# A two-layer transformer kernel: order of the wide weight products, sorted gate and up slots, S5 outputs a slot later, one mask product, and attention's sums by high and low parts

## The reference, cut to what matters

```python
def swiglu(x, w_gate, w_up, w_down):
    return (jax.nn.silu(x @ w_gate) * (x @ w_up)) @ w_down
...
# stick_breaking_attention, 8 heads of 128
z = jnp.einsum('bthd,bshd->bhts', qf[:, q0:kend], kf[:, :kend])
causal = s_idx < t_idx
log_beta = jax.nn.log_sigmoid(z)
log_one_minus = jnp.where(causal, log_beta - z, 0.0)
rest = lax.cumsum(log_one_minus, axis=3, reverse=True) - log_one_minus
w = jnp.where(causal, jnp.exp(log_beta + rest), 0.0)
outs.append(jnp.einsum('bhts,bshd->bthd', w, vf[:, :kend]))
...
# s5_mixer
_, hstate = lax.associative_scan(combine, (a, bu), axis=1)
y = (jnp.einsum('gpn,blgn->blgp', c_re, hstate.real) - jnp.einsum('gpn,blgn->blgp', c_im, hstate.imag) + d_skip * uf)
y = jax.nn.gelu(y.reshape(bsz, L, S5_WIDTH))
y = y * jax.nn.sigmoid(y @ w_glu + b_glu)
```

## Time and profile before

| | |
|---|---|
| median of 3 runs | 1508.41 us (1508.37 to 1508.93) |
| the profiled execution: its time | 1510.64 us |
| its span, first to last instruction | 1508.8 us |
| TensorE matmul busy, share of the span | 1499.7 us, 99% |
| TensorE weight load | 1388.6 us, 92% |
| VectorE (DVE) | 1182.3 us, 78% |
| ScalarE (ACT) | 792.6 us, 53% |
| HBM read | 258.61 MB, 172 GB/s over the span |

### The profile page before, as it was taken

The page is one execution under the profiler, slowest core; times in us unless marked ns, Lnnn a source line. Parts: engine busy times, 40 slices in busy tenths (PEclk is TensorE's granted clock), DMA queues, the critical chain, the costliest instruction groups (busy, mean ns, idle before and its releaser), DMA issues.

```text
span 1508.8 us, 25562 instructions
## 1 busy us (share of the span) xinstructions
PE 1499.7 (99%) x10908; PEld 1388.6 (92%) x10908; DVE 1182.3 (78%) x1560; ACT 792.6 (53%) x1003; POOL 39.4 (3%) x41
## 2 busy tenths in 40 slices
PE   8999999999999999999999999999999999999999
PEld 7888899999988888888889999999999999999989
DVE  7987776797888865988758688889998899766744
ACT  6444455565544443544445556455545745775654
POOL 0000001210000000000001020000000000000000
PEclk9999999999999999999999999999999999999999
DMA  7555545434555545555554444465554453325531
GB/s 283 196 196 195 175 167 184 153 140 150 186 185 187 190 173 200 191 180 185 191 191 149 174 151 157 143 227 194 197 194 172 164 193 131 125 106 189 182 126 56
DMA packets 38976, 261.30 MB, mean 173 GB/s; under 512 B 4688, under 2 KB 5584, under 8 KB 9168
## 3 DMA queue, kind: packets, MB, share of 16 engines
q1 hardware_dynamic: 38000, 258.62, 47.8%
q10 hardware_dynamic: 864, 1.05, 0.2%
HBM read 258.61 MB, written 1.05 MB: 172 GB/s over the span
## 4 chain that ended last, share of the span: by engine, by line
PE 94%; DVE 4%; ACT 1%; DMA 0%; issue 0%; ACTq 0%
PE ps L264 22%; PE ps L211 14%; PE ps L213 14%; PE ps L212 14%; PE ps L266 11%; PE ps L725 8%; PE ps L727 4%; DVE w_low L201 2%; PE ps L1448 1%; DMA w_raw<-in_weights 0%; PE ps L1439 0%; PE ps L1421 0%; ACT w_high L194 0%; DVE scratch L2119 0%; PE ps L1463 0%; PE ps L2264 0%
## 5 line engine op out<-in xcount | busy, mean ns | idle before, releaser
L194 ACT ACTIVATE w_high<-w_raw 128x2048 fp32r<-128x2048 f32 (+2 forms) x244 | 459.8, 1886 | 423.2 <-PE ps L266 188.1
L201 DVE TENSOR_TENSOR w_low<-w_raw,w_high 128x2048 fp32r<-128x2048 f32 (+2 forms) x244 | 552.8, 2267 | 127.3 <-ACT w_high L194 125.3
L264 PE MATMUL ps<-x,w_high 128*128 128x512 f32 x1408 | 498.4, 399 | 2.5 <-DVE w_low L878 2.5
L266 PE MATMUL ps<-x,w_low 128*128 128x256 f32 x1408 | 394.8, 280 | 0.0
L264 PEld LDWEIGHTS ps<-x,w_high 128*128 128x128 f32 x1408 | 265.2, 188 | 67.2 <-DVE x L817 2.8
L266 PEld LDWEIGHTS ps<-x,w_low 128*128 128x128 f32 x1408 | 266.3, 189 | 0.1
L211 PE MATMUL ps<-x,w_high 128*128 128x256 f32 x904 | 261.0, 289 | 0.2 <-DVE x L302 0.2
L213 PE MATMUL ps<-x,w_low 128*128 128x256 f32 x904 | 255.7, 283 | 0.0
L212 PE MATMUL ps<-x,w_high 128*128 128x256 f32 x904 | 255.6, 283 | 0.0
L725 PE MATMUL ps<-ffn_hid,w_high 128*128 128x512 f32 x528 | 183.2, 390 | 0.0
L211 PEld LDWEIGHTS ps<-x,w_high 128*128 128x128 f32 x904 | 173.1, 192 | 5.1 <-issue 3.9
(11 more groups left out here) (456 smaller groups left out, 2359.4 us busy)
## 6 DMA issues: line engine op xcount, KB each, us to landing
w_raw<-in_weights SPq DMA_DIRECT2D x231, 1024.0 KB, 4.8
w_raw<-in_weights SPq DMA_DIRECT2D x10, 768.0 KB, 4.2
w_raw<-in_weights SPq DMA_DIRECT2D x5, 512.0 KB, 3.8
even_second_vectors<-in_second SPq DMA_DIRECT2D x1, 1836.0 KB, 7.2
resid<-in_x SPq DMA_DIRECT2D x3, 256.0 KB, 6.5
w_raw<-in_weights ACTq DMA_DIRECT2D x3, 256.0 KB, 8.0
out<-resid SPq DMA_DIRECT2D x3, 256.0 KB, 2.4
table<-in_table SPq DMA_DIRECT2D x1, 737.0 KB, 8.3
```

Source lines behind the costliest of these rows:

```text
L194: act.activation(self.wh[:, j, 0:SIZES[n]], self.raw[:, j, 0:SIZES[n]], ACT.Copy).then_inc(self.hi_made, 1)
L201: dve.tensor_tensor(self.wl[:, j, 0:SIZES[n]], self.raw[:, j, 0:SIZES[n]], self.wh[:, j, 0:SIZES[n]].bitcast(F32), ALU.subtract).then_inc( ...
L264: pe.matmul(c.bank(bank + i).rearrange("p (a t) -> p a t", a=2), wh[:, k, f], c.x[:, :, k, :], start=(k == 0), stop=False, skip_group_chec ...
L266: mm = pe.matmul(c.bank(bank + i, SEQ), wl[:, k, f], c.xh[:, k, :], start=False, stop=(k == DT - 1), skip_group_check=True)
```

## The change

1. `wide`: a slot without a norm, from the third slot on, first runs its 16 matmuls of `w_high` (512 columns) and then its 16 of `w_low` (256 columns). It waits for `hi_made` before the first half and for `lo_made` before the second; `midway` is run between the halves.
2. `A_Y`: the first two S5 outputs move one slot back, from behind slots 6 and 8 to behind 7 and 9.
3. `scores`: the two mask products of 128 columns a head become one of 256.
4. `suffixes`: DVE's `lost` now also makes a high and a low part of the lost part (two more instructions, the first behind a wait for the previous pair's sums); the constant matrices are copied once into fp32r (`tri`, `minus`, two more DVE instructions). A head's sums are six fp32r matmuls in place of three float32 ones (six in the profile).
5. `suffixes(p)` moves from behind slot 15 + p into the middle of slot 16 + p, behind `spread`; ACT does `logs` before `weights`.
6. The low part uses the room of `yl`, so `gelu_low` waits for the last pair's sums, and it stands behind `after(n)` and `attention_low` in DVE's iteration 18.

```diff
--- before.py
+++ after.py
@@ -245,7 +245,23 @@
 def wide(c, pe, bank, n, norm=None, midway=None):
 
 
     wh, wl = c.weights_at(n, DT, FC)
+    if n > 1 and not norm:
+        pe.wait_ge(c.hi_made, c.made(n))
+        for k in range(DT):
+            for i in range(2):
+                pe.matmul(c.bank(bank + i).rearrange("p (a t) -> p a t", a=2), wh[:, k, i * P:(i + 1) * P], c.x[:, :, k, :],
+                          start=(k == 0), stop=False, skip_group_check=True)
+        pe.wait_ge(c.lo_made, c.made(n))
+        for k in range(DT):
+            if midway and k == 0:
+                midway()
+            for i in range(2):
+                mm = pe.matmul(c.bank(bank + i, SEQ), wl[:, k, i * P:(i + 1) * P], c.xh[:, k, :], start=False,
+                               stop=(k == DT - 1), skip_group_check=True)
+        return mm
     if n > 1:
         pe.wait_ge(c.lo_made, c.made(n))
     for k in range(DT):
@@ -1716,7 +1732,7 @@
 A_ATT, A_SUFFIX, A_PV = 14, 15, 17
 A_S5 = (2, 3, 5, 6, 8, 9, 11, 12)
 A_IN = {2: (0, 2), 5: (2, 2), 8: (4, 1), 9: (5, 1), 11: (6, 1), 12: (7, 1)}
-A_Y = (6, 8, 11, 14)
+A_Y = (7, 9, 11, 14)
 QK_SLOTS, PAIRS = 8, SB_HEADS // 2
 
 EVEN_UNITS = ([(n, 0, "dve") for n in range(A_V)] + [(n, 0, "act") for n in range(A_V, A_GLU)]
@@ -1753,6 +1769,7 @@
         self.decay, self.turn, self.gain = sb("decay", [P, S5_TILES]), sb("turn", [P, S5_TILES]), sb("gain", [P, DT])
         self.qg, self.half_bg = sb("q_gain", [P, 1]), sb("half_b_glu", [P, UT])
         self.ident, self.mask = sb("ident", [P, P], F32R), sb("mask", [P, 2, P], F32R)
+        self.tri, self.minus = sb("tri", [P, P], F32R), sb("minus", [P, P], F32R)
         self.ss = sb("q_sums", [P, 2, 4])
         self.mix, self.first = sb("both_means", [P, SEQ]), sb("first_rstd", [P, SEQ])
         self.cos = sb("cos", [P, S5_TILES, HALF])
@@ -1773,6 +1790,7 @@
         logs = (self.rot[:, 0:6 * P], self.b[:, :, :, :].rearrange("p a c n -> p (a c n)")[:, 0:6 * P])
         self.logs = [t.rearrange("p (h t) -> p h t", h=2) for t in logs]
         self.w = [self.cos[:, 6 * i:6 * i + 6, :].rearrange("p a t -> p (a t)").rearrange("p (h t) -> p h t", h=2) for i in range(2)]
+        self.lost = [t.rearrange("p a t -> p (a t)")[:, 0:6 * P].rearrange("p (h t) -> p h t", h=2) for t in (self.obh, self.yl)]
         self.gate = self.rot[:, :].rearrange("p (a t) -> p a t", a=UT)
         self.vec_in, self.gain_made, self.sq_made, self.sum_made, self.mix_made, self.rooted, self.first_made, self.h_made = (
             c.sem(f"even_{n}") for n in ("vec_in", "gain_made", "sq", "sum", "mix_made", "first_root", "first", "resid_normed"))
@@ -1824,6 +1842,8 @@
             dve.tensor_scalar(e.qg[:, :], E[:, E_QG:E_QG + 1], SB_SCALE, None, ALU.mult)
             dve.tensor_scalar(e.half_bg[:, :], E[:, E_BG:E_BG + UT], 0.5, None, ALU.mult)
             dve.tensor_scalar(e.ident[:, :], c.tab[:, T_IDENT:T_IDENT + P], 1.0, None, ALU.mult)
+            dve.tensor_scalar(e.tri[:, :], c.tab[:, T_TRI:T_TRI + P], 1.0, None, ALU.mult)
+            dve.tensor_scalar(e.minus[:, :], c.ones[:, 4, :], 1.0, None, ALU.mult)
             dve.tensor_scalar(e.mask[:, :, :], c.tab[:, T_STRICT:T_STRICT + P].unsqueeze(1).to_broadcast([P, 2, P]), 1.0, -NEG,
                               ALU.subtract, ALU.mult)
             dve.tensor_tensor(e.gain[:, :], c.vec[:, V_N1:V_N1 + DT], E[:, E_NORM:E_NORM + DT], ALU.mult).then_inc(e.gain_made, 1)
@@ -2046,10 +2066,10 @@
                 value(n)
             if 0 <= n - A_ATT < PAIRS:
                 act.preload_act_table_set("natural_log_exp_and_others")
+            if 0 <= n - A_ATT < PAIRS:
+                logs(n - A_ATT)
             if 0 <= n - A_SUFFIX < PAIRS:
                 weights(n - A_SUFFIX)
-            if 0 <= n - A_ATT < PAIRS:
-                logs(n - A_ATT)
             if n == A_GLU - 2:
                 gelu()
             if 0 < n < A_GLU - 1:
@@ -2132,10 +2152,13 @@
         def lost(p):
 
 
-            l = e.logs[p % 2]
+            l, (high, low) = e.logs[p % 2], e.lost
             dve.wait_ge(self.logged, p + 1)
-            dve.scalar_tensor_tensor(out=l, in0=self.score_banks(p), scalar=0.0, in1=l, op0=ALU.max,
-                                     op1=ALU.add).then_inc(self.lost_made, 1)
+            ln(dve.scalar_tensor_tensor(out=l, in0=self.score_banks(p), scalar=0.0, in1=l, op0=ALU.max, op1=ALU.add))
+            if p:
+                dve.wait_ge(self.suffix_made, p)
+            ln(dve.tensor_scalar(high, l, 1.0, None, ALU.mult))
+            dve.tensor_tensor(low, l, high.bitcast(F32), ALU.subtract).then_inc(self.lost_made, 1)
 
         def gated(p):
             h = slice(2 * p, 2 * p + 2)
@@ -2162,6 +2185,7 @@
 
         def gelu_low():
             dve.wait_ge(self.y_high, 1)
+            dve.wait_ge(self.suffix_made, PAIRS)
             dve.tensor_tensor(e.yl[:, :, :], e.u[:, :, :], e.yh[:, :, :].bitcast(F32), ALU.subtract).then_inc(self.y_low, 1)
             dve.wait_ge(self.y_low, 1)
             ln(dve.scalar_tensor_tensor(out=e.u[:, :, :], in0=e.u[:, :, :], scalar=0.5, in1=e.zb, op0=ALU.mult, op1=ALU.mult))
@@ -2185,14 +2209,14 @@
                 gated(n - A_PV)
             if 0 <= n - A_ATT < PAIRS:
                 lost(n - A_ATT)
-            if n == A_GLU - 2:
-                gelu_low()
             if n:
                 after(n)
             if n in A_S5 and n != A_Q:
                 scan(A_S5.index(n))
             if n >= A_PV:
                 attention_low(n - A_PV)
+            if n == A_GLU - 2:
+                gelu_low()
             if n == A_V - 1:
                 self.norm.first(dve)
             if n in (A_V, A_V + 1):
@@ -2295,20 +2319,29 @@
                 h, z = 2 * p + i, self.score_banks(p)[:, i, :]
                 pe.matmul(z[:, 0:SEQ], e.k[:, h, 0:P], e.q[:, h, :], start=True, stop=False, skip_group_check=True)
                 pe.matmul(z[:, SEQ:3 * P], e.k[:, h, P:SEQ], e.q[:, h, P:SEQ], start=False, stop=False, skip_group_check=True)
-                for a in range(2):
-                    mm = pe.matmul(z[:, 2 * a * P:(2 * a + 1) * P], e.ident[:, :], e.mask[:, a, :], start=False, stop=False,
-                                   skip_group_check=True)
+                mm = pe.matmul(z.rearrange("p (a t) -> p a t", a=3)[:, 0:3:2, :], e.ident[:, :], e.mask[:, :, :], start=False,
+                               stop=False, skip_group_check=True)
             mm.then_inc(self.scored, 1)
 
         def suffixes(p):
-            tri, one = c.tab[:, T_TRI:T_TRI + P], c.ones[:, 4, :]
             pe.wait_ge(self.lost_made, p + 1)
             for i in range(2):
-                z, l = self.score_banks(p)[:, i, :], e.logs[p % 2][:, i, :]
-                pe.matmul(z[:, 0:SEQ], tri, l[:, 0:SEQ], start=False, stop=False, skip_group_check=True)
-                pe.matmul(z[:, P:SEQ], one, l[:, SEQ:3 * P], start=False, stop=False, skip_group_check=True)
-                mm = pe.matmul(z[:, SEQ:3 * P], tri, l[:, SEQ:3 * P], start=False, stop=True, skip_group_check=True)
+                z = self.score_banks(p)[:, i, :]
+                for part in e.lost:
+                    l = part[:, i, :]
+                    pe.matmul(z[:, 0:SEQ], e.tri[:, :], l[:, 0:SEQ], start=False, stop=False, skip_group_check=True)
+                    pe.matmul(z[:, P:SEQ], e.minus[:, :], l[:, SEQ:3 * P], start=False, stop=False, skip_group_check=True)
+                    mm = pe.matmul(z[:, SEQ:3 * P], e.tri[:, :], l[:, SEQ:3 * P], start=False, stop=part is e.lost[1],
+                                   skip_group_check=True)
             mm.then_inc(self.suffix_made, 1)
+        def between(n):
+            if 0 <= n - A_Q - 2 < QK_SLOTS:
+                spread(n - A_Q - 2)
+            if 0 < n - A_SUFFIX <= PAIRS:
+                suffixes(n - A_SUFFIX - 1)
 
         def values(p):
             pe.wait_ge(self.w_made, p + 1)
@@ -2325,13 +2358,10 @@
 
         for n in range(A_GLU):
             b = bank_free(even_unit(n))
-            j = n - A_Q - 2
             project(c, pe, b, base + n, DT, norm=None if n else self.norm, tokens=n >= A_Q,
-                    midway=(lambda: spread(j)) if 0 <= j < QK_SLOTS else None).then_inc(c.done, 1)
+                    midway=lambda: between(n)).then_inc(c.done, 1)
             if n == 1:
                 self.norm.mean(pe)
-            if 0 <= n - A_SUFFIX < PAIRS:
-                suffixes(n - A_SUFFIX)
             if n in A_Y:
                 s5_out(A_Y.index(n))
             if n in A_IN:
```

## The result

The changed kernel takes 1511.72 us (median of 17 runs, 1510.05 to 1512.72), the kernel before, run beside it, 1508.37 us (17 runs, 1505.6 to 1509.71). The ratio is 1.002, 95% interval 1.0013 to 1.0027: slower by 3.35 us, small but clear. The forecast of 1505.6 us had the wrong sign; the range of 1498 to 1513 holds the time.

The account below looks back on a forecast made before the run. TensorE's matmuls, covering 99% of the span, were taken as the bound. The terms -6.5 - 1.1 - 1.0 - 1.3 + 5.5 + 1.6 = -2.8 us, put on the median of 1508.41, gave 1505.6 us; range 1498 to 1513.

Parts of the forecast that it names:

- part 1: Sorted wide slots: 512-column matmuls at 0.227 us, 5.55 us a slot, 61 slow slots gain 0.107 us each: -6.5 us.
- the waits before `scores`: Attention: sums half a slot later leave time enough for `scores(2)` and `scores(3)`, so no wait: 0.
- the base: Whole kernel: the -2.8 us was put on the median of 1508.41 us, taken as about the profiled span, 1508.8.
- the clock: TensorE behind the pause before the GLU: a lowered clock costs half of 3.4 us, +1.6 us (0 to 3.4).
- the case's own upper end: Whole kernel: the likeliest case (chance 0.55) ranged from 1503 to 1508 us, with a half run at 0.225 to 0.232.
- the slow beat stays: Rival for the wide slots: sorted slots keep 0.233 us for 512 columns, gaining 0; 1512.1 us, chance 0.25.
- without a pause: Rival before the GLU: `yl` comes in time, 5.5 and 1.6 us are saved; 1498.5 us, chance 0.10.
- with a spoilt beat: Rival for the wide slots: fast ones slow down too, 0.1 us on 83 slots and more; near 1520 us, chance 0.03.
- The third rival: Wide slots: 512-column runs stream at 0.215 us, a slot takes 5.36 us; 1490 us, chance 0.07.
- Parts 2 and 3: S5 outputs a slot later lose their wait, -1.1 us; one mask product of 256 columns a head, -1.0 us.
- Part 4: Attention sums in fp32r: 12 matmuls a pair, 1.44 us in place of 1.75: -1.3 us (-0.9 to -1.5).
- Parts 5 and 6: Before the GLU: `yl` comes 9.6 us behind the last sums against 4.1 of cover; TensorE idles +5.5 us (4.5 to 6).

Follow-up runs that it names:

- act_order_2: `gelu_back` with ACT's last two `columns` and exponentials of pairs 0 to 2 behind the logarithms, the last exponential behind gelu: 1502.77 us, ratio 0.9957.
- gelu_back: The changed kernel with `gelu_low` put back ahead of the split of slot 21 in DVE's queue: 1506.97 us, ratio 0.999 to the kernel before.
- no_wide: The changed kernel with `wide` as it was before: 1514.24 us, ratio 1.0045 to the kernel before.
- s5_only: The kernel before with only the first two S5 outputs moved a slot later: one profiled execution, 1504.69 us.
- before_third: The kernel before, unchanged, profiled once more: 1507.46 us.
- before_fourth: The kernel before, unchanged, profiled once more after `before_third`: 1510.27 us.

## Why the prediction was right or wrong

Predicted on the profile, against the two profiled executions by start times, us:

| term | predicted | measured |
|---|---|---|
| sorted wide slots | -6.5 | -4.5 |
| S5 outputs | -1.1 | -0.9 |
| masks | -1.0 | -0.7 |
| sums in fp32r | -1.3 | -1.5 |
| waits before `scores(2)`, `scores(3)` | 0 | +1.95 |
| pause before the GLU | +5.5 | +5.3 |
| clock | +1.6 | +2.3 |
| sum | -2.8 | +2.0 (spans: +2.0) |

On the medians the change is +3.35, another 1.35 us: 2.2 because the profiled execution of before was above its median, less 0.9 by which the changed kernel's was.

So the forecast is 6.1 us off by several steps, and no single one turned the sign: 2.0 by the size of part 1, 1.95 by the waits before `scores` that were put at 0, 1.35 by the base, 0.7 by the clock, the rest small. With the waits alone put right, the forecast would still have been below the kernel before, and likewise with the base alone.

**The base, the first step that failed.** "The median of the runs is 1508.41, about the span. The difference goes on the median." But every run listed with its span is about 1.8 us above it, so the span that belongs to a median of 1508.4 is 1506.6, and the profiled 1508.8 was 2.2 us above the typical one. The excess of 1510.64 over the median stood in the prediction and was put down to what lies around the span; by the experiments, mostly some 20 slow slots (20 x 0.1 us) more than usual. That share is inferred and not counted: only four executions of the kernel before were profiled, and the start adds to the spread. But on the medians the sorted slots bring 2.5 us, between the profiles 4.5, and 6.5 was forecast.

**Part 1, the term that was mis-sized.** The sorted slots did leave the slow beat, and the steady 5.57 us stands in all FFNs of all seven kernels that break the alternation. Two sizes were off. The 512-column matmul is not 0.227 us throughout: the first five of a run start 0.228 to 0.236 us apart, and a slot is 5.57 us, not 5.55, 0.02 us on each of 83 slots, of which the 22 fast ones become slower. By this the case's own upper end of 1508 us was too low: at the 0.232 us that it names, a slot is 5.63 us, 61 slots gain 1.3 us and 22 lose 1.9, part 1 is about +0.6, and the time some 1512.7. The first FFN took 0.55 us more, 0.3 to 0.4 of it from this on its fast slots; the rest lies in its first slots and I didn't trace it further. The rival "the slow beat stays" gave 1512.1 us, near the result, and was nevertheless wrong in its mechanism: the beat didn't stay. The rivals without a pause and with a spoilt beat fall by the same rows.

**The third rival.** The sorted first half takes 3.65 us, 228 ns a matmul and not 215, so the rival of 1490 us falls. The formula in the Trainium skill ("TensorE: Matmul & The Clock Gate", Back-to-back issue gap) gives 215.7 ns for 512 columns, and 3.45 us for a first half. That section gives it for a single matmul in isolation, and for a stream of weight loads and matmuls of 512 columns it has about 131 ns. This trace, which is such a stream, agrees with neither, and for fp32r at this shape the measurement decides.

**Parts 2 and 3.** The wait at the S5 output went as said. The masks gave 0.17 us a pair by themselves and some 0.05 at the product behind, in place of 0.25; where `scores` follow a wait, their first product gives 0.08 of it back. The reason: the one product of 256 columns starts 0.20 us before its successor, not 0.12, so a part of the old 0.26 was the change of type, as the bound allowed.

**Part 4, the second step that failed.** The sums themselves came out (about 1.4 us a pair against 1.75; the prediction's own 7.0 - 5.8 is 1.2 and not 1.3). The sentence that failed is that `scores(2)` and `scores(3)` "need the exponentials of pairs 0 and 1, which end about 1.2 and 2 us ahead". I followed only what reads the moved step directly. The exponential was in time; what stood behind it on ACT, a split and `columns`, was not, and that too is read by `scores`. It cost 1.95 us; `act_order_2` shows that an order without it exists.

**Parts 5 and 6.** The best of the prediction: 9.5 us behind the sums (9.6 said), 4.1 us of cover (4.1), a pause of 5.3 (5.5). That most of it hangs on DVE's order is what `gelu_back` shows: a pause of 1.4 us is left, 1.7 were forecast for that order.

**The clock.** Right in kind, 0.7 us too small for the profiled execution: 6.9 us at the low level, 5.24 of them in dense work, 2.3 us lost against 1.6. I had halved 3.4 us, the stretch that a wait of 2.5 us left behind at the start; the pause is twice as long, and the loss lies between the value taken and the upper end that I gave (3.4). It varies, 2.3 us here and 1.4 in `no_wide`, and by the medians filling the pause gave back 1.7. So 1.6 was near the typical loss, with some luck: it was half of one low stretch at the start, which isn't the same in every execution either.

## What to carry to other kernels

Where a profile's span plus its usual overhead is above the median, look for what differs between executions, such as a stretch that keeps two beats, and put a gain from that stretch on the typical execution and not on the profiled one. When an instruction in an in-order queue is made to wait longer, list everything behind it and its readers, not only its own reader. And place what the critical engine waits for next at the head of its maker's queue: one misplaced 1.2 us subtraction cost 4.75 us, 1.7 to 2.3 of it by the clock that sank in the pause.

## What the runs showed of the hardware

- fp32r matmuls alternating one by one between 512 and 256 moving columns run at 0.3467 or at 0.3533 us a couple, for whole FFNs at a time as a rule (in `s5_only` the fourth changes within), and which it is differs between executions of one program. In pairs or in sorted halves they kept 5.57 us for the same 32 in the seven kernels profiled with them.
- The same pause before the GLU, 5.1 us by the list of waits, brought 6.9 us at 1.2 GHz in the changed kernel (1.7 of them still in the pause) and 8 x 0.21 x 2 = 3.4 us in `no_wide` (a window of 8 us from 1348.00 with a clock of 0.79). The wait of 1.4 us there in `gelu_back` left the clock alone. The low stretch at the kernel's start varies likewise: in `before_third` the clock is 1.00 over 12 to 20 us behind a wait of 1.8 us, in `before_fourth` 0.61 behind one of 3.2.
- Plain products of constants in the place of a pause kept the clock at its upper level and gave back 1.7 us; `gelu_back`, with most of the wait gone, is 3.0 us below that.
